# Moving two modulation pieces of a weight stream from the end of one layer to the start of another

## The chip, the core and the metric

One core of a Trainium2 chip runs the whole program. The metric is the device time of one execution in microseconds (us); lower is better. Engine names as the profile has them: PE is the matmul engine (PEld its weight loads), DVE the vector engine, ACT the scalar engine, POOL the third elementwise engine, SP the queue that issues every load here.

## The reference

256 tokens of width 1024 go through four mixers of a first block and two layers of a second block, one after the other:

```python
for i in range(DEPTH):                 # first block: kinds a, b, c, a
    x = x + mixer_i(rms_norm(x, norm_i))
for l in range(DEPTH_2):               # second block
    mod = silu(c) @ w_ada[l] + b_ada[l]             # 6 vectors of 1024
    sh1, sc1, g1, sh2, sc2, g2 = split(mod, 6)
    h = x * (1 + sc1) + sh1
    x = layer_norm(ALPHA * x + g1 * token_mixer(h), ln1)    # m0, m1
    h = x * (1 + sc2) + sh2
    x = layer_norm(ALPHA * x + g2 * conv_ffn(h), ln2)       # f0, f1
```

Mixer c (the short convolution) is `((b * conv3(c*u)) * silu(z)) @ w_out`, with `c, u, b, z` all columns of one product `h @ w_in`. The token mixer begins with `h @ w_in` too, whose columns are, among others, four units of index queries (iq0 to iq3), the index key (ik), a small unit with the index weights and the rotary key (wr), and two latent units (cq0, cq1). The modulation vector `mod` depends on `c` alone, not on `x`: its product can be done anywhere ahead of its use.

## The kernel before, in words

Every weight comes as a piece of 128 x 1024 fp32 values (512 KB) in one stream, whose order `plan()` writes out by hand: mixers a0, b, c, a1, then m0, f0, m1, f1. SP loads the pieces in that order into a ring of six raw buffers: piece i may be loaded once piece i-6 has been used up (`load`). There are three kinds. A **split** piece is turned by ACT into a high half (`feed_act`: a CAST `wh<-raw`), by DVE into a low half (`feed_dve`: a TENSOR_TENSOR `wl<-raw,wh`), in a ring of five buffers; PE then does three products with them, and waits for both halves (`weights`). A **plain** piece goes to PE as it is. An **ada** piece is a piece of `w_ada`: no PE and no ACT, only one SCALAR_TENSOR_TENSOR of DVE with a running sum (`raw<-raw,cb`), which gives one of 48 columns of `mod` for a layer (`ada`).

Every engine's program is written out by hand as well, and each engine works strictly in its own order. Ahead of a unit stands a call `feed_act(name)` or `feed_dve(name)`: it does whatever is not yet done of the pieces up to three behind `name` in the stream (`LOOK = 3`). It counts pieces of all kinds: where two of the next three are ada pieces, it reaches one split piece less far than it would otherwise. At the start of m0, `feed_dve` is called as `feed_dve("m0.wr", 2)`, two pieces ahead.

In mixer c a round handles two blocks of 128 channels (i and i+1; the last round has i = 14). PE makes the c, u, b and z units; for the last z units DVE folds the two parts (`wide`), ACT does the silu, DVE the product y, ACT its high half (`act_high`), DVE its low half (`dve_low`), and PE then adds the product with the pieces c.o14 and c.o15 into the output, which ends the mixer; DVE adds it to x (four residuals), ACT and DVE do the next norm, and a1 begins.

At the start of m0 the order is as follows. PE: the units wr and ik together, iq0, iq1, a tiny product that turns the index weights (`small iw`), iq2, iq3, cq0, cq1. DVE: index weights and rotary key out of the wr unit (done with `rope kr`), `feed_dve(ik)`, the copy of the turned index weights (which waits for PE's tiny product), `feed_dve` of iq0, iq1 and so on. ACT: `feed_act(wr)`, two copies of a gain (`act_gain`), a wait for `rope kr` and a broadcast of it (`KM`, 32x2048), `feed_act(ik)`, the copy of the ik unit, `feed_act` of iq0 and iq1, and the copy of the units iq0 and iq1, which waits for PE to end iq1.

Of the kernel before, what the change touches and what calls it, by code (L numbers as in the profile page):

```python
# [193 lines left out]
def tiles(name, layer, c0, n=128, kt=8):  # L194
    return [(name, layer, 128 * k, 128, c0, n) for k in range(kt)]


def ada_piece(l, u):
    return (f"ada{l}.{u}", [("w_ada_2", l, 128 * u, 128, 0, D, True)], "ada")
# [54 lines left out]
def plan_c(u, u1):  # L254
    out = []

    def ada():
        a = next(u, None)
        out.append(ada_piece(1, next(u1)) if a is None else ada_piece(0, a))

    for i in range(0, 16, 2):
        if i == 0:
            for n in range(2):
                for kind, base in (("c", 2 * E), ("u", 0)):
                    out.append((f"c.{kind}0.{n}", tiles("c_w_in", 0, base + n * 128), "split"))
                    if kind == "u":
                        ada()
        for kind, base in (("c", 2 * E), ("u", 0), ("b", E), ("z", 3 * E)):
            if i == 0 and kind in "cu":
                continue  # L270
            if kind == "z" and i >= 2:
                out.append((f"c.o{i - 2}", [("c_w_out", 0, 128 * (i - 2), 128, 0, D)], "split"))
                ada()
            for n in range(2):
                out.append((f"c.{kind}{i}.{n}", tiles("c_w_in", 0, base + (i + n) * 128), "split"))
            if kind == "z" and i >= 2:
                out.append((f"c.o{i - 1}", [("c_w_out", 0, 128 * (i - 1), 128, 0, D)], "split"))
                ada()
            ada()
    for k in (14, 15):  # L280
        out.append((f"c.o{k}", [("c_w_out", 0, 128 * k, 128, 0, D)], "split"))
    assert next(u, None) is None
    return out
# [5 lines left out]
def plan_m(l, u):  # L289
    M, w, out = f"m{l}", "w_in_2", []  # L290

    def one(name, blocks):
        out.append((f"{M}.{name}", blocks, "split"))

    def ada():
        a = next(u, None)
        if a is not None:
            out.append(ada_piece(1, a))

    one("wr", [x for k in range(8) for x in [(w, l, 128 * k, 128, O_IW, 64), (w, l, 128 * k, 128, O_KR, 32),  # L300
                                             (w, l, 128 * k, 128, O_KR + 16, 16), (w, l, 128 * k, 128, O_KR, 16)]])
    one("ik", [x for k in range(8) for x in [(w, l, 128 * k, 128, O_IK, 64)] * 2])
    for n in range(4):
        one(f"iq{n}", tiles(w, l, O_IQ + 128 * n))
    for n in range(2):
        one(f"cq{n}", tiles(w, l, O_CQ + 128 * n))
    one("ckv", tiles(w, l, O_CKV))
    for n in range(8):
        one(f"qk{n}", tiles(w, l, 128 * n))
        ada()  # L310

    def va(kp):
        one(f"va{kp}", [(w, l, 128 * k, 128, 1024, 512) for k in (2 * kp, 2 * kp + 1)])

    for kp in range(2):
        va(kp)
    for g in range(2):
        heads = range(4 * g, 4 * g + 4)
        one(f"uq{g}", [("w_uq_2", l, 128 * k, 128, 96 * h + a, 16) for k in range(2) for h in heads for a in (80, 64)]
            + [("w_uq_2", l, 128 * k, 128, 96 * h, 96) for h in heads for k in range(2)])  # L320
    for kp in range(2, 4):
        va(kp)
    one("ukv", [("w_ukv_2", l, 0, 128, 128 * h, 64) for h in range(8)]
        + [("w_ukv_2", l, 0, 128, 128 * h + 64, 64) for h in range(8)])
    for n in range(18):
        if n < 16:
            one(f"g{n}", tiles(w, l, (O_GB if n < 8 else O_GA) + 128 * (n % 8)))
        if n in (11, 13, 15, 17):
            one(f"bf{n - 11}", [("w_branch_b_2", l, 128 * k, 128, 128 * v, 128) for v in (n - 11, n - 10)
                                for k in range(4)])  # L330
    for n in range(0, 8, 2):
        one(f"bs{n}", [("w_branch_a_2", l, 128 * k, 128, 128 * v, 128) for v in (n, n + 1) for k in range(4)])
        if n >= 2:
            for k in (n - 2, n - 1):
                one(f"o{k}", [("w_out_2", l, 128 * k, 128, 0, D)])
    for k in (6, 7):
        one(f"o{k}", [("w_out_2", l, 128 * k, 128, 0, D)])
    return out
# [27 lines left out]
def plan():  # L366
    b, u = plan_b()
    u1 = iter(range(48))
    out = plan_a(0) + b + plan_c(u, u1) + plan_a(1)
    u = u1  # L370
    for l in range(2):
        out += plan_m(l, u) + plan_f(l, u)
    assert next(u, None) is None
    return out
# [2641 lines left out]
```

How the kernel before makes its waits and increments, by code:

```python
    def wait_ge(self, sem, value):  # L98
        if self.e is not None and self.seen.get(sem.name, 0) < value:
            self.seen[sem.name] = value
            self.e.wait_ge(sem, value)
# [321 lines left out]
    def load(self, sp, i):  # L423
        if i >= NRAW:
            j = i - NRAW
            if self.kind[j] == "split":
                sp.wait_ge(*self.s["cast"][j])
                sp.wait_ge(*self.s["low"][j])
            elif self.kind[j] == "plain":
                sp.wait_ge(*self.s["gemm"][j])
            else:
                sp.wait_ge(*self.s["ada"][j])
        sp.dma_start(self.raw(i), self.wdram[:, self.off[i]:self.off[i + 1]]).then_inc(self.raw_sems[i % NRAW], 16)
# [1 line left out]
    def sp_program(self, e):  # L435
# [6 lines left out]
        for i in range(2):  # L442
            self.load(sp, i)
        sp.dma_start(self.m["C"][:, NFIRST:NCONST], cst[:, NFIRST:NCONST]).then_inc(s["const"].sem, 16)
        for i in range(2, NRAW):
            self.load(sp, i)
        sp.dma_start(self.m["cb"][:], cbr).then_inc(s["cb"].sem, 16)
        for i in range(NRAW, len(self.pieces)):
            name = self.pieces[i][0]
            for l in range(2):
                if name == f"m{l}.o4":
                    sp.wait_ge(*s["score"][f"m{l}", 15])
                    self.load_ln(sp, f"m{l}")
                if name == f"f{l}.u16.0.0":
                    sp.wait_ge(*s["poolconv"][f"m{l}", 1, 1])
# [54 lines left out]
    def weights(self, pe, name):  # L510
        i = self.at[name]
        pe.wait_ge(*self.s["cast"][i])
        pe.wait_ge(*self.s["low"][i])
```

## Time and profile before

| | us |
|---|---|
| median of 3 runs | 1755.38 |
| lowest, highest | 1754.99, 1758.14 |
| the profiled execution, in whole | 1757.02 |
| its span, first to last instruction | 1755.1 |
| PE busy | 1723.7 (98%) |
| DVE busy | 1477.8 (84%) |
| ACT busy | 1093.9 (62%) |

PE is busy for nearly the whole span, so what counts is where PE stands still, and what it waits for there. The profile follows one execution; PE's busy time of a stretch is the sum of its matmuls, with overlaps counted once. Mixer c ends at about 731 us of the span, a1 runs from there to about 949 us, and m0 from there to about 1150 us.

### The profile page before, as it was taken

How to read it: one execution, taken by the hardware profiler on the slowest of the kernel's cores; microseconds unless marked ns; L12 is line 12 of the kernel's file. 1: busy time of each engine (PE TensorE's matmuls, PEld its weight loads, DVE VectorE, ACT ScalarE, POOL GpSimd, SP SyncE). 2: the span in 40 equal slices, each digit the busy share in tenths (PEclk: the TensorE clock that was granted, in tenths of full speed). 3: DMA queues.
4: the chain of work that ended last, by engine and by line, in shares of the span. 5: the costliest groups of instructions: out<-in, count | busy, mean ns of one | idle time of the engine just before them, and what ended most of it. 6: DMA issues, size and time to landing. Idle time of an engine off the chain costs nothing.

```text
span 1755.1 us, 28782 instructions
## 1 busy us (share of the span) xinstructions
PE 1723.7 (98%) x10458; PEld 1510.9 (86%) x10458; DVE 1477.8 (84%) x2862; ACT 1093.9 (62%) x2150; POOL 289.3 (16%) x396
## 2 busy tenths in 40 slices
PE   9999999999999999999999999999999999999997
PEld 8888888888888888788898988988888998988886
DVE  7998878877789999888987698789987688789887
ACT  6888665555455555577876455566566656566664
POOL 3996000000000000088920000002000200002000
PEclk9999999999999999999999999999999999999999
DMA  6455568855559888544465654546764544546662
GB/s 240 153 157 174 168 220 304 268 177 184 201 195 315 292 301 309 177 151 144 145 196 157 233 172 133 172 150 187 258 218 144 168 156 130 172 144 187 221 187 78
DMA packets 92734, 339.49 MB, mean 193 GB/s; under 512 B 10288, under 2 KB 10672, under 8 KB 91952
## 3 DMA queue, kind: packets, MB, share of 16 engines
q1 hardware_dynamic: 92592, 337.64, 59.1%
q8 instruction: 84, 1.38, 0.3%
q14 instruction: 58, 0.48, 0.1%
HBM read 336.55 MB, written 1.05 MB: 192 GB/s over the span
## 4 chain that ended last, share of the span: by engine, by line
PE 74%; DVE 12%; ACT 8%; issue 4%; POOL 2%; ACTq 0%; DVEq 0%; POOLq 0%
PE ps L104 72%; DVE wl L120 4%; ACT tmp L110 3%; ACT wh L113 2%; POOL B L120 2%; PE ps L107 2%; DVE tmp L130 1%; DVE raw L130 1%; DVE tmp L120 1%; DVE B L120 1%; ACT os L113 1%; DVE sm L142 1%; DVE os L120 1%; ACT B L110 0%; DVE tmp L125 0%
## 5 line engine op out<-in xcount | busy, mean ns | idle before, releaser
L104 PE MATMUL ps<-XS,wh 128*128 128x256 f32 (+2 forms) x3184 | 780.7, 328 | 8.5 <-DVE wl L120 4.4
L120 DVE TENSOR_TENSOR wl<-raw,wh 128x1024 fp32r<-128x1024 f32 x471 | 576.6, 1238 | 101.4 <-ACT wh L113 99.1
L104 PE MATMUL ps<-XS,wl 128*128 128x256 f32 x2152 | 583.1, 282 | 0.0
L104 PEld LDWEIGHTS ps<-XS,wh 128*128 128x128 f32 (+1 forms) x3184 | 527.0, 191 | 64.9 <-issue 19.0
L113 ACT CAST wh<-raw 128x1024 fp32r<-128x1024 f32 x471 | 479.3, 1044 | 100.3 <-PE ps L104 92.8
L104 PEld LDWEIGHTS ps<-XS,wl 128*128 128x128 f32 x2152 | 409.4, 190 | 11.4
L120 POOL TENSOR_TENSOR B<-B,tmp 128x236 f32<-128x236 f32 (+11 forms) x368 | 247.0, 712 | 640.0 <-ACT tmp L110 625.1
L104 PE MATMUL ps<-wh,os 128*128 128x512 f32 x864 | 280.2, 392 | 4.1 <-DVE os L120 2.8
L130 DVE SCALAR_TENSOR_TENSOR ps<-B,C,ps 128x253 f32<-128x253 f32 (+17 forms) x560 | 216.5, 472 | 2.8 <-ACT ps L110 2.8
L104 PE MATMUL ps<-B,raw 128*128 128x256 f32 x992 | 218.6, 380 | 0.0
L104 PEld LDWEIGHTS ps<-B,raw 128*128 128x128 f32 x992 | 187.0, 190 | 27.2 <-issue 2.9
L104 PEld LDWEIGHTS ps<-wh,os 128*128 128x128 f32 x864 | 162.2, 188 | 38.0 <-DVE os L120 4.2
L110 ACT ACTIVATE B<-ps 128x256 f32<-128x256 f32 (+2 forms) x216 | 95.2, 451 | 157.8 <-PE ps L104 157.5
L104 PE MATMUL ps<-wh,XS 128*128 128x512 f32 x576 | 179.5, 391 | 0.0
L110 ACT ACTIVATE tmp<-B,C 128x236 f32<-128x236 f32 (+11 forms) x368 | 153.8, 478 | 34.7 <-POOL B L120 33.9
L104 PE MATMUL ps<-wl,os 128*128 128x512 f32 x432 | 168.3, 390 | 0.0
L120 POOL TENSOR_TENSOR X<-X,B 128x512 f32<-128x512 f32 x24 | 42.1, 1755 | 701.8 <-PE ps L104 701.8
L104 PEld LDWEIGHTS ps<-wh,XS 128*128 128x128 f32 x576 | 107.2, 188 | 21.6
L130 DVE SCALAR_TENSOR_TENSOR raw<-raw,cb 128x1024 f32<-128x1024 f32 x96 | 116.5, 1219 | 0.0
L104 PE MATMUL ps<-wl,XS 128*128 128x512 f32 x288 | 112.4, 390 | 0.0
L104 PEld LDWEIGHTS ps<-wl,os 128*128 128x128 f32 x432 | 81.3, 188 | 16.5
L130 DVE SCALAR_TENSOR_TENSOR tmp<-ps,C,tmp 128x254 f32<-128x254 f32 (+1 forms) x176 | 76.1, 476 | 10.9 <-ACT tmp L110 8.8
(168 smaller groups left out, 1659.7 us busy)
## 6 DMA issues: line engine op xcount, KB each, us to landing
raw<-in_w SPq DMA_DIRECT2D x628, 512.0 KB, 4.4
B<-in_ln SPq DMA_DIRECT2D x4, 1024.0 KB, 7.7
C<-in_cst SPq DMA_DIRECT2D x1, 1103.5 KB, 9.0
X<-in_x SPq DMA_DIRECT2D x2, 512.0 KB, 4.5
out_x<-X SPq DMA_DIRECT2D x4, 256.0 KB, 2.5
cb<-in_cb SPq DMA_DIRECT2D x1, 512.0 KB, 13.6
pos<-in_pos SPq DMA_DIRECT2D x1, 160.0 KB, 5.3
raw<-in_w SPq DMA_DIRECT2D x1, 128.0 KB, 2.0
```

The costliest lines, as they stand in the source:

```text
L104: return NOTHING if self.e is None else self.e.matmul(*a, **k)
L107: return NOTHING if self.e is None else self.e.transpose(*a)
L110: return NOTHING if self.e is None else self.e.activation(*a, **k)
L113: return NOTHING if self.e is None else self.e.copy(*a)
L120: return NOTHING if self.e is None else self.e.tensor_tensor(o, a, b, op)
L130: return self.e.scalar_tensor_tensor(out=o, in0=a, scalar=s, in1=b, op0=op0, op1=op1, **k)
L142: return NOTHING if self.e is None else self.e.tensor_reduce(o, a, AX, ALU.max)
```

## The change

Two of the three ada pieces that stand around the last z units in the stream of mixer c (columns 32 and 33 of the second layer's `mod`) are taken out there and stand instead behind m0.iq0 and behind m0.iq1. No other piece changes its place relative to its neighbours, no instruction is added or taken away, and the programs of the engines are the same text; only the stream's order, and with it what `feed_act`, `feed_dve` and SP do when, is another.

```diff
                 out.append((f"c.o{i - 1}", [("c_w_out", 0, 128 * (i - 1), 128, 0, D)], "split"))
+                if i < 14:
+                    ada()
+            if kind != "z" or i < 14:
                 ada()
-            ada()
...
     for n in range(4):
         one(f"iq{n}", tiles(w, l, O_IQ + 128 * n))
+        if l == 0 and n < 2:
+            ada()
```

The stream around both places, before and after:

```
before  c.o12 ada31 c.z14.0 c.z14.1 c.o13 ada32 ada33 c.o14 c.o15 a1.g0.0 a1.g0.1 a1.v0.0
after   c.o12 ada31 c.z14.0 c.z14.1 c.o13 c.o14 c.o15 a1.g0.0 a1.g0.1 a1.v0.0
before  a1.o15 m0.wr m0.ik m0.iq0 m0.iq1 m0.iq2 m0.iq3 m0.cq0 m0.cq1 m0.ckv
after   a1.o15 m0.wr m0.ik m0.iq0 ada32 m0.iq1 ada33 m0.iq2 m0.iq3 m0.cq0 m0.cq1 m0.ckv
```

## Rows read from the trace of the kernel before

**Rows 1.** Stretches of the span: us, busy time by engine (instructions), PE clock, DMA share, GB/s.

```profile
735.00:945.00 210.00, 210.00 (x1266) 182.18 (x1265) 187.37 (x397) 164.74 (x351) 123.71 (x184) 1.00 0.51 160
```

**Rows 2.** DMA issues of the page: KB each, median us from issue to landing.

```profile
raw<-in_w SPq DMA_DIRECT2D x628, 512.0 KB, 4.4
```

**Rows 3.** DVE in time order, end of mixer c: start, duration, what, [idle before <- releaser].

```profile
717.12 1.22 DVE L130 SCALAR_TENSOR_TENSOR raw<-raw,cb 128x1024 f32<-128x1024 f32 x1
...
719.41 0.42 DVE L120 TENSOR_TENSOR B<-ps,B 128x256 f32<-128x256 f32 x1
721.25 1.23 DVE L120 TENSOR_TENSOR wl<-raw,wh 128x1024 fp32r<-128x1024 f32 x1 [1.42 <-ACT wh L113]
722.39 0.42 DVE L120 TENSOR_TENSOR tmp<-tmp 128x256 f32<-128x256 f32 x1
723.28 0.42 DVE L120 TENSOR_TENSOR os<-tmp,os 128x256 fp32r<-128x256 f32 x1 [0.47 <-ACT os L113]
...
729.58 2.47 DVE L120 TENSOR_TENSOR X<-X,ps 128x512 f32<-128x512 f32 x4
```

**Rows 4.** ACT in time order, end of mixer c.

```profile
712.26 1.04 ACT L113 CAST wh<-raw 128x1024 fp32r<-128x1024 f32 x1
716.63 0.39 ACT L110 ACTIVATE B<-ps 128x256 f32<-128x256 f32 x1 [3.33 <-PE ps L104]
719.86 0.42 ACT L110 ACTIVATE tmp<-B 128x256 f32<-128x256 f32 x1 [2.84 <-DVE B L120]
720.18 1.03 ACT L113 CAST wh<-raw 128x1024 fp32r<-128x1024 f32 x1
```

**Rows 5.** PE in time order, end of mixer c.

```profile
713.13 0.39 PE L104 MATMUL ps<-wh,os 128*128 128x512 f32 x1
...
721.76 0.39 PE L104 MATMUL ps<-wh,os 128*128 128x512 f32 x1
723.75 0.50 PE L104 MATMUL ps<-wh,os 128*128 128x512 f32 x1 [1.61 <-DVE os L120]
...
727.96 0.50 PE L104 MATMUL ps<-wh,os 128*128 128x512 f32 x1 [1.20 <-DVE os L120]
```

**Rows 6.** ACT in time order, start of m0.

```profile
958.29 1.05 ACT L113 CAST wh<-raw 128x1024 fp32r<-128x1024 f32 x1
...
962.01 1.92 ACT L110 ACTIVATE B<-tmp 32x2048 f32<-32x2048 f32 x1 [1.70 <-DVE tmp L120]
963.95 1.05 ACT L113 CAST wh<-raw 128x1024 fp32r<-128x1024 f32 x1
```

**Rows 7.** DVE in time order, start of m0.

```profile
962.01 1.22 DVE L120 TENSOR_TENSOR wl<-raw,wh 128x1024 fp32r<-128x1024 f32 x1
965.03 1.23 DVE L120 TENSOR_TENSOR wl<-raw,wh 128x1024 fp32r<-128x1024 f32 x1 [1.80 <-ACT wh L113]
967.06 0.17 DVE L133 COPY sm<-ps 128x16 f32<-128x16 f32 x1 [0.80 <-PE ps L104]
967.15 4.62 DVE L120 TENSOR_TENSOR wl<-raw,wh 128x1024 fp32r<-128x1024 f32 x4
```

**Rows 8.** PE in time order, start of m0 (iq1, the tiny product, iq2).

```profile
963.38 0.48 PE L104 MATMUL ps<-XS,wh 128*128 128x256 f32 x2
...
966.41 0.61 PE L104 MATMUL ps<-C,tmp 8*128 8x8 f32 x4
966.95 0.51 PE L104 MATMUL ps<-XS,wh 128*128 128x256 f32 x2
```

**Rows 9.** DVE in time order, later in m0.

```profile
1000.96 1.22 DVE L120 TENSOR_TENSOR wl<-raw,wh 128x1024 fp32r<-128x1024 f32 x1 [1.68 <-ACT wh L113]
```

**Rows 10.** PE in time order, end of a0: its longest wait ahead of the end.

```profile
162.74 0.41 PE L104 MATMUL ps<-B,C 128*32 128x256 f32 x2 [1.94 <-ACT tmp L110]
```

**Rows 11.** Two stretches as in rows 1: behind the wait of rows 10, around those of rows 5.

```profile
163.00:167.00 4.00, 4.00 (x26) 3.69 (x19) 2.43 (x3) 3.63 (x5) 0.00 (x0) 0.57 0.67 200
721.00:731.00 10.00, 7.20 (x32) 5.33 (x31) 6.87 (x11) 5.60 (x11) 0.00 (x0) 1.00 0.59 190
```

## The prediction

> **What bounds the kernel now.** I read the page first: PE is busy for 98% of the span, so a change of order can move the time only where PE stands still. Next the busy times by stretch: in the whole of a1, PE is busy for 210.00 of 210 us [rows 1], so a1 is one unbroken row of matmuls, and whatever its start gains or loses comes out at its end, and at m0's start. Then the engines in order of time at the two places of the change. At the end of mixer c, PE waits twice, 1.61 and 1.20 us, both times for the low half of y [rows 5]; at the start of m0 it runs from unit to unit without a wait of note, but only just: the low half of iq1 is made from 962.01 to 963.24 us and PE begins iq1 at 963.38 [rows 7, 8].
>
> **At the end of mixer c** the change removes two ada pieces. Their cost there is not what it looks like. Each holds DVE for 1.22 us (1.14 from start to start), and the fold of z14.0 comes only behind both, at 719.41 [rows 3], although ACT has its part ready at 717.02 [rows 4]. But `feed_dve` counts pieces: its reach of three, which ended with the two ada pieces, now ends with c.o14 and c.o15. So two low halves (1.14 us each from start to start, as the four at 967.15 show: 4.62 us in all [rows 7]) take the place of the two ada pieces, and the fold stays at about 719.4. What they need is there: c.o14 and c.o15 take the loads' places of the two ada pieces, some 4 us ahead of where they were; ACT casts them right behind c.o13's cast at 712.26 [rows 4], c.o14 once PE has let go of its buffer with the end of c.o12 (713.13 + 0.39 [rows 5]), so that at 1.04 each both are done by 715.6, ahead of ACT's next work at 716.63.
>
> The gain lies behind the fold. Before, both remaining pieces were cast and halved inside the chain that PE waits for: ACT's silu at 719.86, the cast of c.o14 from 720.18, DVE's low half of it at 721.25 after 1.42 us of waiting, and only then y at 722.39, its high half, its low half at 723.28, PE at 723.75 [rows 3 to 5]. With the piece ready, y follows the silu at 720.31, that is 2.08 us earlier, and its low half is ready at about 721.65. PE ends c.o13 at about 722.0 (its last matmul starts at 721.76 and the next one in a row follows 0.23 us later), so the first wait goes: c.o14 starts at 722.0, 1.75 us earlier. The same rows repeat for z14.1 in the trace of before, with the same 1.42 of waiting; without cast and low half its chain has its low half ready at 723.7, while PE works on c.o14 until 724.7: c.o15 starts 3.2 us earlier (727.96 to 724.7) and, with twelve matmuls in a row, ends at about 727.5. DVE's four residuals began late before, at 729.58, held by one more low half, and ended at 732.05 [rows 3]; now the first three run while PE ends, and the last starts when PE does end, at 727.65, and is done at 728.3. The norm behind them (squares on ACT, root, transposes on PE) hangs on the last residual. **Gain: 732.05 - 728.3 = 3.8 us**, on the path, and kept through a1. It can't be more than that by much; less, down to 2.8 (the two waits alone), if the norm's other inputs bind.
>
> **At the start of m0** the change adds an ada piece behind iq0 and one behind iq1, and both shorten the reach of the feeds. First pause: `feed_act(wr)` used to reach iq1 and cast it at 958.29; three behind wr is now the ada piece, so ACT does nothing there. The cast of iq1 falls to `feed_act(ik)`, which stands behind the broadcast that waits for the rotary key, 962.01 to 963.93: it takes the place that iq2's cast had, 963.95 to 965.00 [rows 6]. DVE does the first ada piece meanwhile at 962.01 (hidden: before, it waited 1.80 us there), and iq1's low half from 965.03 to 966.26, where iq2's stood [rows 7]. PE starts iq1 at 966.38 instead of 963.38 [rows 8]: **3.0 us**.
>
> Second pause: `feed_dve(ik)` ends with iq1 now, so iq2's low half comes behind the copy of the index weights, and that copy waits for PE's tiny product, which stands behind iq1. Before: product at 966.41, copy at 967.06, next DVE work at 967.15 [rows 7, 8]. Shifted by 3.0, the copy is at 970.06; then the second ada piece from 970.15 (1.14), iq2's low half from 971.29 (1.23), done at 972.52; PE starts iq2 0.12 later, at 972.64, instead of 966.95. **5.7 us in all, 2.7 of them the second pause.** Nothing else in DVE's queue is in need then (iq3's low half follows 1.14 us later, a unit of PE takes 2.9). The casts of iq2 and iq3 are done by 967.2. The loads are far enough ahead: a slot is free six pieces on, a piece lands 4.4 us after its issue [rows 2]; cq0 now waits for iq0's low half (960) and lands at 964.4, ahead of its cast at 970, and the qk0 piece, which waits for the second ada piece (971.3), lands at 975.7, ahead of its use behind cq1. POOL has no work here.
>
> Does a later wait absorb it? The next place where DVE binds is the selection from about 1000 us on; but DVE's low half at 1000.96 had waited 1.68 us for ACT's cast [rows 9], which follows PE: DVE and ACT run behind PE there and move with it. I count the whole 5.7.
>
> **The clock.** A pause of PE can cost more than itself. After the wait of 1.94 us at 160.8 [rows 10] the granted clock fell to the lower of the two levels, 1.2 GHz, on average 0.57 from 163 to 167 with PE busy throughout: 4 x 0.43 = 1.7 us of work lost [rows 11]. After the waits of 1.61 and 1.20 us at the end of c it stayed at 1.00 [rows 11]. The new pauses, 3.0 and 2.7 us (the second with a tiny product in front of it), are longer than the one that was followed by a fall. A fall costs 1.7 us when PE is busy through all of it, less when part of it lies in the pause itself. For two pauses the bounds are 0 and 3.4 us; I take 2.7, since each pause is much longer than the 1.94 us one and nearer to it than to 1.61. The Trainium skill, "TensorE: Matmul & The Clock Gate", section "Why this matters for your kernels", speaks against the change too, as it asks for no longer pauses between bursts of matmuls, but it sets the harmful length well above 1.94 us, close to that of these two pauses; by it neither need lower the clock, and the sum would be the second rival's. The trace's fall after 1.94 us disagrees, and the row decides.
>
> **The sum.** -3.8 + 5.7 + 2.7 = +4.6 us. The profiled execution took 1757.02 us (span 1755.1 and 1.9 outside it), which lies between the runs' 1754.99 and 1758.14; their median, 1755.38, is 1.6 lower, and execution by execution the clock's falls may differ. Against the profiled one the forecast is 1761.6, against the median **1760.0 us**, and that is what I give.
>
> **The rivals.**
> - *The clock holds* (or falls only where PE pauses anyway). Then -3.8 + 5.7 = +1.9: 1757.3 us, within what can't be told from no change. For it: the waits of 1.61 us had no such effect. Against: rows 10.
> - *The pauses are made good later; faster.* If the selection of m0, which DVE leads from about 1000 us, started at a time that PE's delay doesn't move, the 5.7 us would vanish in it and c's gain would remain: 1755.4 - 3.8 = 1751.6 us. This decides as soon as DVE has 5.7 us of its own backlog at 1000; the 1.68 us that it waits there for ACT speak against it.
> - *The gain at c does not come*: c.o14 or c.o15 not loaded or cast in time, since the DMA engines are busy there. The chain keeps its length, m0 loses as above: +5.7 + 2.7 = +8.4, 1763.8 us. Against it: the pieces move into slots that were served about 4 us earlier.
>
> **Chances.** Forecast, with one or two falls of the clock: 0.65. The clock holds: 0.18. Made good later: 0.07. No gain at c: 0.08. A remainder of 0.02 for the change not doing what it says. Range for 8 in 10: the forecast's own bounds are 1757.3 + 1.2 (one short fall) to 1757.3 + 3.4, with about 1 us either way for the gain at c (2.8 to 3.8) and for the runs' own spread; with the clock-holds case in it, 1756.4 to 1762.6. A measurement of this kernel tells about 0.2%, 3.5 us, from no change. The forecast lies at +4.6, only 1.1 beyond that bound, so about a sixth of its chance falls within: slower 0.53 + 0.08 = 0.61 or a little more, same 0.12 + 0.18 = 0.30 or a little more, faster 0.07.
>
> **What would show it right or wrong.** In the new trace: no wait of PE at c.o14 and c.o15, and the residuals ending 3.8 us earlier; a1 as long as before; PE waiting for DVE's `wl` ahead of iq1 (about 3 us) and of iq2 (about 2.7), with an ada piece of DVE between the index weights' copy and iq2's low half; a granted clock below 1.00 in the few us behind. I am wrong if iq1's cast still stands ahead of the broadcast, if PE waits again at c.o14, or if the two pauses don't show up in the time at which the m0 layer ends.

## The result: 0.29% slower

| | before | after |
|---|---|---|
| median, us (8 runs each) | 1756.2 | 1761.53 |
| lowest to highest, us | 1754.94 to 1758.14 | 1759.76 to 1762.4 |
| the profiled execution, in whole | 1757.02 | 1761.32 |
| its span | 1755.1 | 1759.4 |

The ratio is 1.0029, with a 95% interval of 1.0019 to 1.0038: the median is 5.3 us higher. The forecast was 1760.0 us, 4.6 us above the median of three runs that was known then.

**The end of mixer c after the change.** DVE and PE in order of time (start, duration, what, [idle before <- releaser]), first DVE:

```profile
717.78 0.42 DVE L120 TENSOR_TENSOR B<-ps,B 128x256 f32<-128x256 f32 x1
718.68 0.42 DVE L120 TENSOR_TENSOR tmp<-tmp 128x256 f32<-128x256 f32 x1 [0.48 <-ACT tmp L110]
719.58 0.43 DVE L120 TENSOR_TENSOR os<-tmp,os 128x256 fp32r<-128x256 f32 x1 [0.47 <-ACT os L113]
...
723.92 2.73 DVE L120 TENSOR_TENSOR X<-X,ps 128x512 f32<-128x512 f32 x4
```

Then ACT's casts of c.o13 (one) and of c.o14 and c.o15 (two):

```profile
710.66 1.04 ACT L113 CAST wh<-raw 128x1024 fp32r<-128x1024 f32 x1
712.00 2.00 ACT L113 CAST wh<-raw 128x1024 fp32r<-128x1024 f32 x2 [0.30 <-PE ps L104]
```

And all the waits of PE from 700 to 760 us (total, times, longest):

```profile
PE ps L107 <- DVE tmp L125: 0.2, 1, 0.2
```

The cast of c.o13 stood at 712.26 before [rows 4]: this execution arrives 1.60 us earlier, for a reason that lies ahead of the change (it is given below). From there on: the residuals end at 723.92 + 2.73 = 726.65 against 732.05 [rows 3], 5.40 earlier, so the end of c itself gained **3.8 us**. Fold, product and low half follow each other without cast or low half of a weight between them, and PE's two waits [rows 5] are gone. The remaining wait is that for the norm.

**The start of m0 after the change.** First ACT, the broadcast of the rotary key and the cast of iq1:

```profile
956.57 1.91 ACT L110 ACTIVATE B<-tmp 32x2048 f32<-32x2048 f32 x1 [2.64 <-DVE tmp L120]
958.50 1.04 ACT L113 CAST wh<-raw 128x1024 fp32r<-128x1024 f32 x1
```

DVE: first ada piece, low half of iq1, the copy of the index weights, second ada piece, five low halves from iq2 on:

```profile
956.57 1.23 DVE L130 SCALAR_TENSOR_TENSOR raw<-raw,cb 128x1024 f32<-128x1024 f32 x1
...
959.58 1.23 DVE L120 TENSOR_TENSOR wl<-raw,wh 128x1024 fp32r<-128x1024 f32 x1 [1.78 <-ACT wh L113]
967.14 0.17 DVE L133 COPY sm<-ps 128x16 f32<-128x16 f32 x1 [6.34 <-PE ps L104]
967.24 1.21 DVE L130 SCALAR_TENSOR_TENSOR raw<-raw,cb 128x1024 f32<-128x1024 f32 x1
...
968.37 5.76 DVE L120 TENSOR_TENSOR wl<-raw,wh 128x1024 fp32r<-128x1024 f32 x5
```

PE: iq1, the tiny product, iq2:

```profile
960.95 0.77 PE L104 MATMUL ps<-XS,wh 128*128 128x256 f32 x2 [3.00 <-DVE wl L120]
...
966.35 0.76 PE L104 MATMUL ps<-C,tmp 8*128 8x8 f32 x4
969.74 0.48 PE L104 MATMUL ps<-XS,wh 128*128 128x256 f32 x2 [2.63 <-DVE wl L120]
```

The broadcast is 5.44 us earlier than before (962.01 [rows 6]): a1 kept what c gained. Against before [rows 8], iq1 is 2.43 us earlier, the tiny product 0.06 earlier, iq2 2.79 later. The first pause took 3.0 us, iq1 itself 5.40 us instead of 3.03, and the second pause with the tiny product 3.39 instead of 0.54, 2.85 more. Stretches of after (us, busy time by engine, then PE clock, DMA share, GB/s) show why iq1 is long, and the third one is that of [rows 11] at the end of a0:

```profile
959.00:966.00 7.00, 5.05 (x23) 5.08 (x24) 1.23 (x1) 2.71 (x4) 0.00 (x0) 0.56 0.45 145
970.00:974.00 4.00, 4.00 (x23) 4.00 (x23) 4.00 (x4) 0.00 (x0) 0.00 (x0) 0.57 0.92 313
163.00:167.00 4.00, 4.00 (x39) 3.76 (x32) 2.58 (x4) 3.56 (x5) 0.00 (x0) 1.00 0.70 210
```

The granted clock fell to the lower level (1.2 GHz) in the first pause, stood at 1.00 again from 967.0 to 969.7, and fell once more right behind the second pause. At the end of a0 both kernels have the same code, and there the clock held in this execution: the casts ahead of that place are 0.07 us earlier than before, those behind it 1.57, so 1.5 of the 1.60 us are this. DVE's row of [rows 9] is now

```profile
1005.22 1.23 DVE L120 TENSOR_TENSOR wl<-raw,wh 128x1024 fp32r<-128x1024 f32 x1 [1.68 <-ACT wh L113]
```

which is 4.26 us later than before, and the span ends 4.3 later: nothing behind the pauses made anything good.

The profiled executions add up: -1.6 (ahead of the change, 1.5 of it a0's clock, which is chance) - 3.8 (c) + 3.0 + 2.4 (first pause, slow iq1) + 2.85 (second pause) + 1.5 (slow iq2 and iq3) = +4.35 us, against 4.3 for the spans.

### The profile page after: what moved, and what is told of

Read it like the earlier page. It is cut to its first block, busy times and chain, and to the rows that moved or that the text cites. A ratio compares the mean times of both kernels' runs of the same rounds, so it can differ in the third digit from the quotient of the medians.

```text
span 1759.4 us, 28784 instructions
## 1 busy us (share of the span) xinstructions
PE 1724.5 (98%) x10458; PEld 1511.6 (86%) x10458; DVE 1478.3 (84%) x2862; ACT 1095.0 (62%) x2150; POOL 289.3 (16%) x396
## 4 chain that ended last, share of the span: by engine, by line
PE 73%; DVE 12%; ACT 8%; issue 4%; POOL 2%; DMA 0%; SPq 0%; ACTq 0%; DVEq 0%; POOLq 0%
PE ps L104 72%; DVE wl L120 5%; ACT tmp L110 4%; ACT wh L113 2%; POOL B L120 2%; PE ps L107 2%; DVE tmp L130 1%; DVE raw L130 1%; DVE tmp L120 1%; DVE B L120 1%; ACT os L113 1%; DVE sm L142 1%; DVE tmp L125 1%; ACT B L110 1%; DVE os L120 1%
```

## The experiments

The theory: neither half is about the 1.22 us that an ada piece takes on DVE. At the end of c the pieces took the place of c.o14 and c.o15 in the feeds' reach of three; in m0 they take the place of iq1 and iq2, and the pauses let the clock fall. The rivals: DVE's time of the pieces alone; a clock whose fall is chance alone; a price of the place in the stream as such, loads among it. Executions can differ by the falls of the clock, so for a part of the program the traces are compared from row to row, and for the whole the medians. The kernel before was run again beside them: its median was 1755.65 us for the first four runs below and 1756.84 for the last four. The intervals of the medians are 2.9 to 4.5 us wide, so where two expectations differ by 2 us or less, the rows decide.

**Each half alone.** The end of c alone leaves out the second half of the diff; the start of m0 alone leaves out the first.

```diff
# e1: only the end of c          # e2: only the start of m0
-        if l == 0 and n < 2:    -                if i < 14:
-            ada()               -                    ada()
                                 -            if kind != "z" or i < 14:
                                 +            ada()
```

> The half at the end of mixer c alone: the two ada pieces leave c, the start of m0 keeps its stream, and all later ada pieces move up two places, so that two more stand in f0. My theory (the reach of the feeds): PE no longer waits at c.o14 and c.o15, the residuals end 3.8 us earlier, nothing is lost later: about -3.8 us against before. Rival (only DVE's time of the two pieces counts, 2 x 1.14 us): at most -2.3 us. Rival (DVE in f0 is full, and the pieces cost there what they gave at c): about -1.4 us (-3.8 + 2.4).

Measured: 1752.95 us, ratio 0.9985 (0.9977 to 0.9994), -2.7 us. In the trace, PE has one wait of 0.2 us around the end of c, as in the changed kernel. From the cast of c.o13 (712.26 to 710.54, 1.72 earlier) to the end of the residuals (732.05 to 726.55, 5.50 earlier) the gain is 3.8 us:

```profile
723.82 2.73 DVE L120 TENSOR_TENSOR X<-X,ps 128x512 f32<-128x512 f32 x4
```

Matched row by row with before, 0.4 us are then lost in m0, at about 1015, and 0.7 between 1250 and 1300, in f0, where two more ada pieces stand. The rows put the 0.4 to the numbering, though no run tests it: every eighth column is followed by two short operations of DVE (0.28 us together); at each ada place of m0 there now stands a column two lower, so the two operations behind column 39 come two ada places later, at 1006.90, inside the selection, and PE waits 0.23 us for a low half at 1015.52, which it did not before. So the theory's term at c is right; that nothing is lost later is not. The median alone can't tell -3.8 from the rivals' -2.3 and -1.4 (its interval is -4.0 to -1.1 us); the 3.8 us at c and the 0.7 in f0 rule both out.

> The half at the start of m0 alone: c as before, two ada pieces (then numbers 34 and 35) behind iq0 and iq1, two fewer in f0. My theory: PE waits 3.0 us ahead of iq1 and 2.7 ahead of iq2, +5.7 us, and the clock falls behind one or both pauses, +1.7 to +4.0: in all +7.4 to +9.7 us. Rival (only DVE's time of the pieces counts): +2.4 us at most, since DVE has idle time there. Rival (the clock's fall is chance and belongs to the run): +5.7 us.

Measured: 1764.65 us against 1755.65, ratio 1.0051 (1.0038 to 1.0064), +9.0 us. iq1 starts again after a wait of 3.00 us:

```profile
966.35 0.77 PE L104 MATMUL ps<-XS,wh 128*128 128x256 f32 x2 [3.00 <-DVE wl L120]
```

Against before (963.38 [rows 8]) 3.0 us late, iq2 8.3 late and cq0 9.8 late. The rival of 2.4 us falls, and so does that of a clock whose fall is chance (+5.7): the interval is +6.7 to +11.2 us, and the fastest of the five runs is 7.4 us above the median of before. The halves add up: -2.7 + 9.0 = +6.3, against +5.3 for both; the 1 us between them is inside the intervals.

**The clock's part.** Matmuls of no use into the pauses:

```diff
+            if l == 0 and n in (1, 2):
+                self.warm(pe, 12 if n == 1 else 11, 3)
             self.unit(pe, ps[7 - n // 2][:, (n % 2) * T:(n % 2) * T + T], f"{M}.iq{n}", M)
```

> The changed kernel, with matmuls of no use put into the two pauses of m0: 12 times a 128x128 product ahead of iq1 (2.8 us) and 11 times ahead of iq2 (2.6 us), in a PSUM bank that is free there; nothing else is changed, and PE's waits for the low halves remain. My theory: the pauses stay what they are (5.7 us), the granted clock stays at 1.00 behind them, and the clock's part, 2.7 to 4.0 us, goes: about +1.9 us against before (-3.8 + 5.7). Rival (iq1 and iq2 run long for another reason, such as loads or reads that collide): iq1 still takes about 5.4 us and the time stays at about +5.3.

Measured: 1757.39 us, ratio 1.0010 (1.0001 to 1.0019), +1.7 us against the expected +1.9. iq1, from its start to the tiny product, takes 965.49 - 962.46 = 3.03 us again, and the clock holds from before the first pause until behind the second:

```profile
962.46 0.47 PE L104 MATMUL ps<-XS,wh 128*128 128x256 f32 x2 [0.31 <-DVE wl L120]
...
965.49 0.61 PE L104 MATMUL ps<-C,tmp 8*128 8x8 f32 x4
```

```profile
955.00:975.00 20.00, 19.69 (x164) 19.23 (x163) 12.20 (x16) 9.24 (x11) 0.00 (x0) 1.00 0.58 182
```

The pauses are still there, only filled. From the broadcast of the rotary key to DVE's row of [rows 9] this kernel takes 5.7 us longer than before, the changed one 9.7 (5.44 + 4.26). So the waits' part is 5.7 us and the clock's part 4.0 by the traces; by the medians the clock's part is 5.3 - 1.7 = 3.6, known to about 2.3 us either way. With the clock at 1.00 iq1 takes the time that it took before, so nothing is left for another cause.

**The reach in m0.** The changed stream, with feeds that reach past the ada pieces:

```diff
-        self.feed_act(act, f"{M}.wr")
+        self.feed_act(act, f"{M}.wr", LOOK if l else 4)
...
-        self.feed_act(act, f"{M}.ik")
+        self.feed_act(act, f"{M}.ik", LOOK if l else 5)
...
-        self.feed_dve(dve, f"{M}.ik")
+        self.feed_dve(dve, f"{M}.ik", LOOK if l else 5)
```

> The changed kernel, with the reach of three feeds at the start of m0 (layer 0) lengthened by the ada pieces that they meet: ACT's feed at wr reaches 4, ACT's and DVE's feeds at ik reach 5 pieces. The stream is the changed one. My theory: iq1 is cast at 958 again, DVE does ada, low half of iq1, ada, low half of iq2 behind the rotary key, PE waits about 1.1 us ahead of iq1 and not ahead of iq2, and the clock holds: -3.8 + 1.1 = about -2.7 us against before. Rival (the ada pieces' place in the stream itself costs, by DVE's time or the loads): the pauses remain, about +5.

Measured: 1753.7 us, ratio 0.9988 (0.9979 to 0.9996), -2.0 us. DVE does both ada pieces, in the same place of the stream, between the low halves, and PE waits once:

```profile
958.13 1.23 DVE L130 SCALAR_TENSOR_TENSOR raw<-raw,cb 128x1024 f32<-128x1024 f32 x1
...
959.28 1.22 DVE L120 TENSOR_TENSOR wl<-raw,wh 128x1024 fp32r<-128x1024 f32 x1
960.42 1.22 DVE L130 SCALAR_TENSOR_TENSOR raw<-raw,cb 128x1024 f32<-128x1024 f32 x1
...
961.56 1.22 DVE L120 TENSOR_TENSOR wl<-raw,wh 128x1024 fp32r<-128x1024 f32 x1
```

```profile
960.65 0.47 PE L104 MATMUL ps<-XS,wh 128*128 128x256 f32 x2 [1.13 <-DVE wl L120]
```

The wait of 1.13 us is the first ada piece ahead of iq1's low half: that is all that the place in the stream costs. The other 4.6 us of the pauses went with the longer reach, and the granted clock is 1.00 from 955 to 975 us. The trace is at -2.74 us behind iq2, as expected; the interval of the median is -3.7 to -0.7.

**One piece only**, behind iq1 (the other moves on down the stream):

```diff
-        if l == 0 and n < 2:
+        if l == 0 and n == 1:
```

> The changed kernel with the ada piece behind iq1 only; the other moves down the stream with all later ones (one more in f0). My theory: ACT's feed at wr reaches iq1 again, so the first pause goes; DVE's feed at ik ends with the ada piece, so iq2's low half still stands behind the copy of the index weights, but without an ada piece between: PE waits about 1.5 us ahead of iq2, and iq2 starts 1.5 us late. In the trace, from iq0 to iq2: +1.5 us against before instead of +8.2; against before in all about -3.9 + 1.5 + 0.5 for f0 = -1.9. Rival (both pauses come from the piece's 1.22 us on DVE alone): 1.2 us at most.

Measured: 1755.57 us, ratio 0.9997 (0.9987 to 1.0007): by the median not to be told from the kernel before, nor from the expected -1.9. The first pause is gone, the second is as expected, but the clock fell behind it, which was not expected:

```profile
960.82 0.61 PE L104 MATMUL ps<-C,tmp 8*128 8x8 f32 x4
...
962.91 0.49 PE L104 MATMUL ps<-XS,wh 128*128 128x256 f32 x2 [1.49 <-DVE wl L120]
```

```profile
963.00:967.00 4.00, 4.00 (x22) 4.00 (x23) 4.00 (x4) 1.34 (x2) 0.00 (x0) 0.57 0.69 218
```

From iq1 to iq2 PE loses 1.5 us against before, 1.5 more in iq2 and iq3 at the lower clock, and 0.9 in f0: by the rows, what c gained is gone. So the piece behind iq0 makes the first pause, through ACT's feed, and of the second pause's 2.63 us 1.5 are DVE's feed and 1.1 the time of the piece that stands between the copy and iq2's low half.

**What the end of c gains from.** Two kernels made from the kernel before, one that takes away DVE's time of the two pieces and leaves the reach, one that leaves the time and lengthens the reach:

```diff
# e7: in ada()
-        dve.stt(raw, raw, 1.0, self.m["cb"][:], ALU.mult, ALU.mult, accum_out=md[:, u:u + 1])...
+        wd = 8 if l and u in (32, 33) else D
+        dve.stt(raw[:, 0:wd], raw[:, 0:wd], 1.0, self.m["cb"][:, 0:wd], ALU.mult, ALU.mult, ...)
# e8: in act_c, and the same in dve_c
-                self.feed_act(act, f"c.z{i}.{n}")
+                self.feed_act(act, f"c.z{i}.{n}", 5 if i == 14 and n else LOOK)
```

> The kernel before, in which the two ada pieces of the last round of c are worked on for 8 of their 1024 columns only (two columns of the modulation are left out in their larger part); stream, loads and reach are those of before. It measures what DVE's time of the two pieces is worth at that place. My theory (time and reach act together): the fold of z14.0 comes about 2 us earlier, but the casts and low halves of c.o14 and c.o15 stay in the chain: PE still waits about 1.2 us at c.o15, the residuals end about 2.0 us earlier, about half of the 3.8. Rival (time alone explains it): 3.8 us.

Measured: 1753.68 us, ratio 0.9983 (0.9973 to 0.9993). The cast of c.o13 is at 710.51, 1.75 us earlier than before (1.5 of it by a0's clock); the residuals end at 725.72 + 2.47 = 728.19, 3.86 earlier: the gain at the end of c is 2.1 us. PE still waits at c.o15 (first row; the second has the residuals):

```profile
724.11 0.50 PE L104 MATMUL ps<-wh,os 128*128 128x512 f32 x1 [1.03 <-DVE os L120]
...
725.72 2.47 DVE L120 TENSOR_TENSOR X<-X,ps 128x512 f32<-128x512 f32 x4
```

> The kernel before, with the reach of ACT's and DVE's feeds at z14.1 lengthened from 3 to 5 pieces in the last round of c: both ada pieces and the low halves of c.o14 and c.o15 are all done ahead of the fold of z14.0. My theory: the fold comes 2.3 us later (721.7), the chain behind it is shorter by cast and low half each time, PE's wait at c.o14 stays (about 1.8 us), that at c.o15 goes, and the residuals end about 1.6 us earlier. Rival (reach alone explains it): 3.8 us.

Measured: 1754.01 us, ratio 0.9986 (0.9976 to 0.9996). The cast of c.o13 is at 712.17 (0.09 earlier), the residuals end at 727.64 + 2.70 = 730.34, 1.71 earlier: 1.6 us of gain. PE waits at c.o14 and no longer at c.o15 (again with the row of the residuals):

```profile
723.88 0.50 PE L104 MATMUL ps<-wh,os 128*128 128x512 f32 x1 [1.86 <-DVE os L120]
...
727.64 2.70 DVE L120 TENSOR_TENSOR X<-X,ps 128x512 f32<-128x512 f32 x4
```

Neither alone gives the 3.8 us; 2.1 + 1.6 = 3.7, together they do. Taking the pieces out of the stream there does both at once. So the theory that neither half is about the pieces' time on DVE holds for m0, where 1.1 us are left of 5.7, but not for c, where that time is 2.1 of the 3.8. It is the rows that show this: by the medians both kernels lie within their intervals of 3.8 us (-4.7 to -1.2 and -4.2 to -0.7).

**A version that keeps the gain.** The two pieces leave c, but stand behind cq0 and cq1, where the feeds at wr, ik, iq0 and iq1 don't meet them:

```diff
     for n in range(4):
         one(f"iq{n}", tiles(w, l, O_IQ + 128 * n))
-        if l == 0 and n < 2:
-            ada()
     for n in range(2):
         one(f"cq{n}", tiles(w, l, O_CQ + 128 * n))
+        if l == 0:
+            ada()
```

> The two ada pieces leave mixer c as in the change, but stand behind cq0 and cq1 of m0 instead of behind iq0 and iq1; every later piece stays where the change has it. My theory: the feeds at wr, ik, iq0 and iq1 reach what they reached before, DVE does the two pieces in its idle time of 2.8 and 3.2 us around 972 and 977 us, so nothing is lost in m0, nor in f0, which had 0.7 us too much with two more pieces in the run with the half at c alone: about -3.9 us. Rival (an ada piece costs wherever it stands in m0): -1.5 us or slower.

Measured: 1751.61 us against 1756.84, ratio 0.9971 (0.9961 to 0.9981): 5.2 us less, faster than both kernels. DVE does the pieces between the low halves of cq0 and cq1 and behind the latter, earlier than expected and with 1.64 us to spare behind them:

```profile
963.19 2.35 DVE L120 TENSOR_TENSOR wl<-raw,wh 128x1024 fp32r<-128x1024 f32 x2
965.46 1.22 DVE L130 SCALAR_TENSOR_TENSOR raw<-raw,cb 128x1024 f32<-128x1024 f32 x1
...
966.60 1.22 DVE L120 TENSOR_TENSOR wl<-raw,wh 128x1024 fp32r<-128x1024 f32 x1
967.74 1.22 DVE L130 SCALAR_TENSOR_TENSOR raw<-raw,cb 128x1024 f32<-128x1024 f32 x1
...
970.60 1.23 DVE L120 TENSOR_TENSOR wl<-raw,wh 128x1024 fp32r<-128x1024 f32 x1 [1.64 <-ACT wh L113]
```

PE has no wait for a weight from 945 to 980 us. The span is 1751.2, 3.9 us less than before, with the clock's falls at the same two places as there, at about 163 and 1000 us. The 3.9 are the expected gain; the interval of the medians (-6.9 to -3.3 us) holds it.

## Why the prediction was right

- **The gain at c, 3.8 us:** measured 3.8, by the mechanism named: low halves in the place of the ada pieces, with the fold of z14.0 where it was (719.41 against 717.78 + 1.60) and PE's two waits gone. The later runs divide it: 2.1 us for the pieces' time on DVE, 1.6 for the reach.
- **The first pause, 3.0 us:** 3.00, iq1's cast behind the broadcast and DVE's ada piece in what had been idle time.
- **The second pause, 2.7 us:** 2.63 as the trace counts it, 2.85 from the tiny product to iq2; the ada piece follows the copy of the index weights and iq2's low half follows it.
- **The 5.7 us are not made good later:** right; the shift of 4.26 us at 1005 us is that of the end, 4.3.
- **The clock, 2.7 us, bounds 0 and 3.4:** the term that was mis-sized. It was 3.9 us in the profiled execution (2.4 in iq1, 1.5 behind) and 3.6 by the medians of the changed kernel and the one with filled pauses. The upper bound was too low: the prediction took each fall to cost what it had worked out for the one at 163 us, 1.7 (the rows put that one at 1.5). But the granted clock averaged 0.56 over the seven us from 959 to 966, and iq1 ran all of its time at the lower level, 2.4 us longer; only the second fall, 1.5, was of the size assumed.
- **The rivals:** that the clock holds would have given +1.9 us, and the kernel with filled pauses, where it did hold, is at +1.7; that the pauses are made good, or that c's gain does not come, is ruled out by the rows above.
- **The sum** against the median was +4.6, measured +5.3. The 0.7 between them is inside the interval (+3.3 to +6.7), and that it is so small is partly luck: by the rows the change itself costs 5.9 us (9.7 - 3.8), 1.3 more than forecast, and 1.2 of these are the clock's term. The spans differ by 4.3 and not by 5.9 because the clock held at the end of a0 in one of the two profiled executions, which has nothing to do with the change.

The Trainium skill, "TensorE: Matmul & The Clock Gate", section "Why this matters for your kernels", asks for no pauses of PE beyond a length that lies at about the longest of those seen here. The traces differ: the clock also fell at pauses of 1.49, 1.94 and 2.63 us, as at the one of 3.00. By that rule neither pause need have lowered the clock. (The rival that this comes to, the clock holds, is the first of the prediction's list; the prediction calls it the second.)

## What to carry to other kernels

Where feeds reach ahead by a count of pieces in one stream, a piece moved in or out changes what every feed near it has ready, and that can cost several times the work of the piece itself (here 9.7 us at the start of m0 for two pieces of 1.22): list, for each call, which pieces it reaches before and after. Where an engine's order has a wait on the bound engine (here DVE's copy of the index weights), don't put work that nobody waits for between that wait and the next thing that the bound engine needs; put it further on, where the engine has a lead again, as in the version behind cq0 and cq1. And count a pause of the matmul engine with the fall of the clock that may follow it: here the two falls cost 3.9 us on top of 5.7 of pauses.

## What was not expected of the hardware

The fall of the clock does not go by the length of the pause alone. The wait of PE at the end of a0, 1.78 to 1.98 us long and with the same code in all ten traces, was followed by a granted clock of 0.57 to 0.62 in six of them and of 1.00 in four; a fall there is 1.5 us of the execution.

A second place of the kind stands in m0, and the prediction did not look at it: the clock falls there in the trace of before as well, behind a wait of only 0.79 us, with twelve products of a single column ahead of it. The rows of before are

```profile
1000.04 1.50 PE L104 MATMUL ps<-C,tmp 128*128 128x1 f32 x12 [0.16 <-ACT tmp L110]
1002.33 0.48 PE L104 MATMUL ps<-XS,wh 128*128 128x256 f32 x2 [0.79 <-DVE wl L120]
```

```profile
1000.00:1010.00 10.00, 9.17 (x64) 9.12 (x65) 7.17 (x20) 4.87 (x7) 0.00 (x0) 0.83 0.63 224
```

PE counts as busy for 1.50 of the 2.29 us from 1000.04 to 1002.33, and the clock falls all the same. All ten traces have these two rows, with the same 1.50 and 0.79 us; the clock fell behind them in seven and held in three: with filled pauses, with the longer reach in m0 and with the longer reach in c. A fall there is 1.3 us of an execution (the kernel with filled pauses goes from 1.76 us behind that of before to 0.48). The two places are 2.8 us together, which can account for a good part of the spread of the runs; which of the runs without a trace had which fall is not known.

The pause of 1.49 us behind a tiny product (one piece only) was followed by a fall too. Waits of 1.61 [rows 5] and 1.86 us at the end of c were not: the clock from 721 to 731 us was 1.00 in the kernel with the longer reach there, as in [rows 11]. What decides is left open; no run was made for it.
